# The skip term D times x of a state-space stage: from TensorE to GpSimd

## The chip, the cores and the metric

The kernel runs on one core of a Trainium2 chip. The metric is the device time of one execution in microseconds (us); less is better. The core has five engines that run their own instruction streams and meet at semaphores: PE (TensorE, matrix products), DVE (VectorE), ACT (ScalarE), POOL (GpSimd) and SP (SyncE, which issues most DMAs).

## The reference, cut to what matters

One layer of a hybrid diffusion backbone: attention beside a bidirectional Mamba-2 state-space mixer, then a feed-forward part. Only the mixer's output matters here. `xs` is the convolved input (length l, 8 heads of 64 values), `z` a gate:

```python
y_f, fin_f = ssd_chunked(xs, dt_f, a_f, bm, cm, init_f)
y_b, fin_b = ssd_chunked(flip(xs), flip(dt_b), a_b, flip(bm), flip(cm), init_b)
y = y_f + flip(y_b) + d_skip[:, None] * xs        # d_skip: one number per head
y = y.reshape(b, l, SSM_WIDTH) * silu(z)
return rms_norm(y, g_out), fin_f, fin_b
```

`ssd_chunked` splits the sequence into chunks of 128 tokens. A chunk's result has a part from inside the chunk (a 128x128 matrix of weights per head, times x) and a carried part (C times the state that enters the chunk, scaled by a decay per token). There are 1,024 latent tokens and 256 prompt tokens, so 10 chunks.

## The kernel before, in words

The stage is in `phase_front`. It works on one chunk `c` at a time, 0 to 9, with 128 tokens on the partitions and 512 channels (8 heads of 64) along the free axis. All arithmetic is float32. Each engine has its own loop over `c`, in an order written out by hand; there is no planner. The lines of the profile are those of kernel.py.

Before this loop there is a stage over the same chunks that makes the gate z (PE lines L373 to L375) and sweeps the backward state down the sequence. It ends with the semaphore `s_ready`, after which DVE, POOL and PE begin chunk 0.

**PE**, for chunk c: the carried parts, forward into bank A[1] and backward into A[2] (L1407, one semaphore `off_done` for both); the exponents of chunk c+1 (`segments`, L1368 and L1370); the chunk's contribution to the next state (L1347), which overwrites A[1] and so waits for `off_f_read`; the scores C B of chunk c+1 (L1391); then, after `y_ready` of chunk c-1, the four products of x with a diagonal matrix of D (L1419), which begin the sum in bank A[3]; eight products of the weights with x on top of them (L1422, `diag_done`); and the transposes of the normalised chunk c-1 (`y_turn`, L1376), which wait for ACT.

**DVE**, for chunk c: `yv` = A[1] times the forward decay (L1137); `off_b` = A[2] times the backward decay (L1139); `yv += off_b` (L1143); `next_state`, the decayed state plus A[1] (L1129), which waits for PE L1347 and for POOL's `decayed`; `weights_in_chunk` of chunk c+1, a sum and a product of 1,024 elements in a partition (L1116, which waits for ACT's exponential, and L1119); then `yv += A[3]` (L1150) and `yv *= z` (L1151), which gives `y_ready`. Of these, L1116, L1119, L1143 and L1151 have both inputs in SBUF; L1137, L1139, L1129 and L1150 have one in PSUM.

**POOL**, for chunk c: `weigh` (L696), x times the forward weights, free to start when PE has read the old one; `decay` (L675), which waits for `y_ready` of chunk c-1; `rstd` of chunk c-1 (L680 and L681, a power of one element); and `load_u` (L687), a DMA it issues itself.

**ACT**, for chunk c: the sum of squares of chunk c-1 (L860, after `y_ready`); the exponential of chunk c+1 (L871, after the exponents); a copy of the scores (L873); the scaling of chunk c-1 by `rstd` (L865, after POOL L681); and the copy of the transposed chunk back to SBUF (L877).

**SP** stores each finished chunk and loads rows for attention. When all engines are done, the attention phase begins.

The diagonal matrices `ddiag` are made by ACT, once, in the stage before (L845). `Chain.link` marks an instruction with a semaphore and makes its own engine wait for it.

Of the kernel before, what the change touches and what calls it, by code (L numbers as in the profile page):

```python
# [23 lines left out]
P = 128  # L24
# [3 lines left out]
ALU = mybir.AluOpType  # L28
ACT = mybir.ActivationFunctionType
# [6 lines left out]
NT = T // P  # L36
# [8 lines left out]
SH, SP_, DS = 8, 64, 128  # L45
SW = SH * SP_
# [3 lines left out]
N_XBC, N_Z = 8, 4  # L50
# [19 lines left out]

C_GPRE, C_GFFN, C_BMOD, C_GQ, C_GKV, C_CW, C_CB, C_GS, C_DB, C_AL, C_DS = 0, 8, 16, 64, 67, 69, 93, 101, 105, 121, 137
N_COLS = 141

# [312 lines left out]
def phase_front(L):  # L386
# [6 lines left out]
    with ExitStack() as st:  # L393
# [18 lines left out]
        def at(name, home, skip, shape, dt=F32):  # L412

            return nc.alloc_sbuf_tensor_at(name, shape, dt, offset=L.home[home] + skip)
# [9 lines left out]
        maskb = at("maskb", "conv_acc", 0, [P, 2, 4, P], BF16)  # L424
        ddiag = at("ddiag", "conv_acc", 2048, [P, 4, P])
        identb = at("identb", "conv_acc", 4096, [P, P], BF16)
# [30 lines left out]
        def turn_bank(n):  # L457
# [22 lines left out]
         s_ready, cb_done, cb_read, seg_done, exp_done, off_done, off_f_read, off_b_read, w_ready, diag_done, y_ready, squared,  # L480
         rstd_ready, yn_ready, y_turned, mix_ready, sf_ready, dec_ready, fin_mm, fin_cp, consts, pch) = (
             L.sem("ss_" + n) for n in (
                 "ones", "xwf_ready", "st_loaded", "st_turned", "sch", "z_done", "z_copied", "x_turned",
                 "x_copied", "xw_ready", "s_mm", "s_ready", "cb_done", "cb_read", "seg_done", "exp_done", "off_done",
                 "off_f_read", "off_b_read", "w_ready", "diag_done", "y_ready", "squared", "rstd", "yn_ready", "y_turned", "mix_ready",
                 "sf_ready", "dec_ready", "fin_mm", "fin_cp", "consts", "pch"))
        block = st.enter_context(nc.Block())
# [46 lines left out]
        per_head = lambda ap: ap.rearrange("p (a r) -> p a r", r=2).unsqueeze(3).to_broadcast([P, 4, 2, SP_])  # L534
        dskip = L.cols[:, C_DS:C_DS + 4]
        up2 = L.up2
# [19 lines left out]
        def _(sp):  # L556
# [39 lines left out]
            for d in range(2):  # L596
                sp.dma_start(st_in[:, d, :, :], L.dram["state_ssm"][0, 0, d].rearrange("(a h) p n -> (h p) a n", a=4)
                             ).then_inc(st_loaded, 16)

            sp.wait_ge(z_done, NT)  # L600
            for dst, name in ((L.table, "rope_table"), (L.wq_raw, "w_uq"), (L.wk_raw, "w_uk"), (L.wv_raw, "w_uv")):
# [18 lines left out]
        def _(pool):  # L620
# [72 lines left out]
            def weigh(c):  # L693

                pool.wait_ge(s_mm, NS + c)
                pool.tensor_tensor(heads4(quads(xw[:, 0, :])), heads4(xs(c)), per_head(wgt[:, c, 0:8]), ALU.mult  # L696
                                   ).then_inc(xwf_ready, 1)

            pool.wait_ge(s_ready, NS)
            for c in range(NT):  # L700
                weigh(c)
                decay(c)
                if c >= 1:
                    rstd(c - 1)
                if c + 2 < NT:
                    load_u(c + 2)
# [3 lines left out]
        def _(act):  # L710
# [118 lines left out]
            def constants(i):  # L829

                if i < 2:
                    act.activation(pick[0:64, i, :, :], across(L.const[0:64, K_SEL:K_SEL + 16], P), ACT.Copy,
                                   scale=-1.0).then_inc(consts, 1)
                elif i < 4:
                    d = i - 2
                    act.activation(maskb[:, d, :, :], L.const[:, K_MASK + d * P:K_MASK + (d + 1) * P]
                                   .unsqueeze(1).to_broadcast([P, 4, P]), ACT.Copy).then_inc(consts, 1)
                elif i == 4:
                    act.activation(identb[:], L.ident, ACT.Copy).then_inc(consts, 1)
                elif i == 5:  # L840
                    act.activation(up2[64:66, :], L.ones[64:66, 0:1].to_broadcast([2, T]), ACT.Copy
                                   ).then_inc(ones_set, 1)
                elif i == 6:
                    for a in range(4):
                        act.activation(ddiag[:, a, :], L.ident, ACT.Copy, scale=dskip[:, a:a + 1]).then_inc(consts, 1)  # L845

# [46 lines left out]
        def _(dve):  # L893
# [239 lines left out]
            for c in range(NT):  # L1133
# [7 lines left out]
                dve.wait_ge(off_f_read, c + 1)  # L1141
                dve.wait_ge(off_b_read, c + 1)
                f.link(dve.tensor_tensor(yv[:, c % 2, :], yv[:, c % 2, :], off_b[:], ALU.add))  # L1143

                if c + 1 < NT:
                    next_state(c)
                    weights_in_chunk(c + 1)

                dve.wait_ge(diag_done, c + 1)
                f.link(dve.tensor_tensor(yv[:, c % 2, :], yv[:, c % 2, :], A[3], ALU.add))  # L1150
# [8 lines left out]
        def _(pe):  # L1159
# [218 lines left out]

            pe.wait_ge(consts, 9)
            pe.wait_ge(ones_set, 1)  # L1380
# [19 lines left out]
            for c in range(NT):  # L1400
# [15 lines left out]
                if c >= 1:  # L1416
                    pe.wait_ge(y_ready, c)
                for a in range(4):
                    pe.matmul(A[3][:, chunk(a)], L.xbcT[:, a, chunk(c)], ddiag[:, a, :], start=(a == 0), stop=False)  # L1419
                pe.wait_ge(w_ready, c + 1)  # L1420
                for h in range(SH):
                    mm = pe.matmul(A[3][:, h * SP_:(h + 1) * SP_], wt[:, c % 2, h, :],  # L1422
                                   xs(c)[:, h // 2, (h % 2) * SP_:(h % 2 + 1) * SP_], start=False, stop=(h == SH - 1))
                mm.then_inc(diag_done, 1)
# [1874 lines left out]
```

## Time and profile before

| | us |
|---|---|
| median of 3 runs (1698.46 to 1698.77) | 1698.68 |
| the profiled execution, its time | 1697.26 |
| the profiled execution, its span | 1695.4 |
| PE busy | 1635.9 (96%) |
| DVE busy | 988.7 (58%) |
| ACT busy | 682.1 (40%) |
| POOL busy | 77.7 (5%) |

The profile is one execution. Times count from the start of its span. In a row of the timeline the first number is when an instruction began, the second how long it took; then the engine, the line, the operation, what it wrote and read, and its shape. An idle time that stood before it is in brackets, with what ended it. An instruction that began and then had to wait for something inside the chip shows a longer duration, not an idle time. PE's instructions overlap, so for PE the distance between two starts says more than a duration. In a row of the windows, each pair is an engine's busy time in that stretch and its count of instructions, in the order PE, weight loads of PE, DVE, ACT, POOL, followed by PE's granted clock as a share of 2.4 GHz, the DMA share and GB/s.

### The profile page before, as it was taken

How to read it: one execution, taken by the hardware profiler on the slowest of the kernel's cores; microseconds unless marked ns; L12 is line 12 of the kernel's file. 1: busy time of each engine (PE TensorE's matmuls, PEld its weight loads, DVE VectorE, ACT ScalarE, POOL GpSimd, SP SyncE). 2: the span in 40 equal slices, each digit the busy share in tenths (PEclk: the TensorE clock that was granted, in tenths of full speed). 3: DMA queues.
4: the chain of work that ended last, by engine and by line, in shares of the span. 5: the costliest groups of instructions: out<-in, count | busy, mean ns of one | idle time of the engine just before them, and what ended most of it. 6: DMA issues, size and time to landing. Idle time of an engine off the chain costs nothing. (4 is left out here: it accounts for less than half of the span.)

```text
span 1695.4 us, 24882 instructions
## 1 busy us (share of the span) xinstructions
PE 1635.9 (96%) x9795; PEld 1450.6 (86%) x9795; DVE 988.7 (58%) x1562; ACT 682.1 (40%) x1188; POOL 77.7 (5%) x116
## 2 busy tenths in 40 slices
PE   6899999999899999989999999999999999999997
PEld 4787878878788888878888999999999999888886
DVE  4653644258755645564588455545555555466788
ACT  4532112335543535454564333333333333434453
POOL 1101000034100000000100000000000000000011
PEclk9999999999999999999999999999999999999999
DMA  9323441013300000214312222222222225763355
GB/s 371 141 97 142 157 151 51 1 52 91 87 7 14 13 1 2 106 42 164 118 69 79 82 87 105 78 91 90 97 89 80 104 80 195 228 226 101 119 168 188
DMA packets 76291, 176.35 MB, mean 104 GB/s; under 512 B 10352, under 2 KB 26944, under 8 KB 74128
## 3 DMA queue, kind: packets, MB, share of 16 engines
q1 hardware_dynamic: 72080, 169.75, 28.9%
q0 software_dynamic: 4096, 5.01, 0.9%
q8 instruction: 79, 1.29, 0.3%
q14 instruction: 36, 0.29, 0.1%
HBM read 131.02 MB, written 43.70 MB: 103 GB/s over the span
## 5 line engine op out<-in xcount | busy, mean ns | idle before, releaser
L373 PE MATMUL psF<-gv,gu_ring 128*128 128x320 f32 x1224 | 379.3, 310 | 3.8 <-DVE gv L2659 3.1
L374 PE MATMUL psF<-gv,gu_ring 128*128 128x320 f32 x1224 | 378.8, 310 | 0.0
L375 PE MATMUL psF<-gv,gu_ring 128*128 128x320 f32 x1224 | 378.8, 309 | 0.0
L373 PEld LDWEIGHTS psF<-gv,gu_ring 128*128 128x128 f32 x1224 | 230.5, 188 | 4.7 <-issue 3.6
L374 PEld LDWEIGHTS psF<-gv,gu_ring 128*128 128x128 f32 x1224 | 230.4, 188 | 0.0
L375 PEld LDWEIGHTS psF<-gv,gu_ring 128*128 128x128 f32 x1224 | 230.4, 188 | 0.0
L373 PE MATMUL psF<-d_w_ring,d_hid_ring 128*128 128x512 f32 x360 | 140.2, 389 | 0.0
L374 PE MATMUL psF<-d_w_ring,d_hid_ring 128*128 128x512 f32 x360 | 140.1, 389 | 0.0
L375 PE MATMUL psF<-d_w_ring,d_hid_ring 128*128 128x512 f32 x360 | 140.0, 389 | 0.0
L373 PE MATMUL psP<-hT_hi,win_hi 128*128 128x512 f32 (+1 forms) x336 | 124.2, 370 | 2.7 <-DVEq L1064 1.5
L375 PE MATMUL psP<-hT_hi,win_lo 128*128 128x512 f32 (+1 forms) x336 | 119.6, 356 | 0.0
L374 PE MATMUL psP<-hT_lo,win_hi 128*128 128x512 f32 (+1 forms) x336 | 119.3, 355 | 0.0
L2459 ACT ACTIVATE hraw<-psF 128x320 f32<-128x320 f32 x130 | 56.6, 437 | 149.8 <-PE psF L375 147.4
L2709 DVE TENSOR_TENSOR hraw<-hraw,psF 128x320 f32<-128x320 f32 x132 | 63.4, 485 | 41.1 <-ACT hraw L2459 35.2
L1788 DVE TENSOR_TENSOR pt_lo<-psPT,pt_hi 128x512 fp32r<-128x512 f32 (+1 forms) x104 | 58.3, 581 | 40.7 <-ACT pt_hi L1664 40.7
L373 PEld LDWEIGHTS psF<-d_w_ring,d_hid_ring 128*128 128x128 f32 x360 | 67.6, 188 | 14.3 <-DVE hraw L2898 0.5
L2501 ACT ACTIVATE d_hid_ring<-d_hid 128x640 fp32r<-128x640 f32 x54 | 40.0, 740 | 98.7 <-PE psF L375 98.0
L374 PEld LDWEIGHTS psF<-d_w_ring,d_hid_ring 128*128 128x128 f32 x360 | 67.6, 188 | 14.1
L375 PEld LDWEIGHTS psF<-d_w_ring,d_hid_ring 128*128 128x128 f32 x360 | 67.6, 188 | 14.1
L2455 ACT ACTIVATE gu_ring<-raw_gu 128x512 fp32r<-128x512 f32 x65 | 40.9, 629 | 95.8 <-PE psF L375 95.8
L373 PEld LDWEIGHTS psP<-hT_hi,win_hi 128*128 128x128 f32 x336 | 63.8, 190 | 17.6 <-issue 4.6
L2766 DVE TENSOR_TENSOR d_hid_ring<-d_hid,d_hid_ring 128x640 fp32r<-128x640 f32 x54 | 44.5, 824 | 53.6 <-ACT d_hid_ring L2501 53.4
(434 smaller groups left out, 3385.7 us busy)
## 6 DMA issues: line engine op xcount, KB each, us to landing
hid_variants<-hraw SPq DMA_DIRECT2D x77, 320.0 KB, 2.2
d_hid<-hid_variants SPq DMA_DIRECT2D x58, 320.0 KB, 3.0
m_wring<-in_w_mod SPq DMA_DIRECT2D x16, 1024.0 KB, 4.9
d_b<-in_w_down SPq DMA_DIRECT2D x44, 256.0 KB, 4.2
win_raw<-in_w_in SPq DMA_DIRECT2D x18, 512.0 KB, 5.7
w_mod_staged<-in_w_mod SPq DMA_DIRECT2D x16, 512.0 KB, 14.7
d_hid_more<-hid_variants SPq DMA_DIRECT2D x19, 320.0 KB, 3.1
raw_gu<-in_w_gate SPq DMA_DIRECT2D x11, 512.0 KB, 3.9
```

What stands on the lines that cost most here:

```text
L373: pe.matmul(out, w_hi, x_hi, start=first, stop=False, skip_group_check=onto)
L374: pe.matmul(out, w_hi, x_lo, start=False, stop=False, skip_group_check=onto)
L375: return pe.matmul(out, w_lo, x_hi, start=False, stop=last, skip_group_check=onto)
L1788: dve.tensor_tensor(pt_lo[:, g[0]:g[-1] + 1, r:r + P], psPT[:, (g0 + i) % 2, 0:len(g), :], pt_hi[:, g[0]:g[-1] + 1, r:r + P].bitcast(F32), ...
L2455: act.activation(w_slot(q)[:, 0, :], block_of(r, n), ACT.Copy).then_inc(wv_hi, 1)
L2459: act.activation(dst[:, chunk(c)], psA(n, c), ACT.Copy).then_inc(copied, 1)
L2501: act.activation(ring_h(e, 0), hr[e % HR], ACT.Copy).then_inc(h_hi, 1)
L2709: dve.tensor_tensor(dst[:, chunk(c)], src[:, chunk(c)], bank(c), ALU.add).then_inc(added, 1)
L2766: dve.tensor_tensor(ring_h(e, 1), hr[e % HR], ring_h(e, 0).bitcast(F32), ALU.subtract).then_inc(h_lo, 1)
```

## The change

The four products with the diagonal matrix leave PE, and with them `ddiag` and ACT's four instructions that make it. POOL makes `dx` = D times x by two more operations of 512 elements in each chunk: `skip(c)`, the product, between `weigh(c)` and `decay(c)`, and `add_skip(c)`, which adds it onto `off_b` once DVE has written that. D is loaded by a small DMA of SP, eight numbers to every partition. On DVE, L1143 now waits for the sum (`skip_added`) and stands behind the next state and the next weights.

```diff
@@ SP @@
+            sp.wait_ge(conv_read, N_XBC)
+            sp.dma_start(dskip[:], L.dram["d_skip"].to_broadcast([P, 8])).then_inc(skip_loaded, 16)
             sp.wait_ge(z_done, NT)
@@ POOL @@
+            def skip(c):
+                p.link(pool.tensor_tensor(heads4(quads(dx[:])), heads4(xs(c)), per_head(dskip[:]), ALU.mult))
+            def add_skip(c):
+                pool.wait_ge(off_b_read, c + 1)
+                pool.tensor_tensor(off_b[:], off_b[:], dx[:], ALU.add).then_inc(skip_added, 1)
             pool.wait_ge(s_ready, NS)
+            pool.wait_ge(x_copied, 2 * NT)
+            pool.wait_ge(skip_loaded, 16)
             for c in range(NT):
                 weigh(c)
+                if c >= 1:
+                    pool.wait_ge(skip_added, c)
+                skip(c)
                 decay(c)
+                add_skip(c)
                 if c >= 1:
                     rstd(c - 1)
@@ ACT @@
-                elif i == 6:
-                    for a in range(4):
-                        act.activation(ddiag[:, a, :], L.ident, ACT.Copy, scale=dskip[:, a:a + 1]).then_inc(consts, 1)
@@ DVE @@
                 dve.wait_ge(off_f_read, c + 1)
-                dve.wait_ge(off_b_read, c + 1)
-                f.link(dve.tensor_tensor(yv[:, c % 2, :], yv[:, c % 2, :], off_b[:], ALU.add))
                 if c + 1 < NT:
                     next_state(c)
                     weights_in_chunk(c + 1)
+                dve.wait_ge(skip_added, c + 1)
+                f.link(dve.tensor_tensor(yv[:, c % 2, :], yv[:, c % 2, :], off_b[:], ALU.add))
                 dve.wait_ge(diag_done, c + 1)
@@ PE @@
                 if c >= 1:
                     pe.wait_ge(y_ready, c)
-                for a in range(4):
-                    pe.matmul(A[3][:, chunk(a)], L.xbcT[:, a, chunk(c)], ddiag[:, a, :], start=(a == 0), stop=False)
                 pe.wait_ge(w_ready, c + 1)
                 for h in range(SH):
-                    mm = pe.matmul(..., start=False, stop=(h == SH - 1))
+                    mm = pe.matmul(..., start=(h == 0), stop=(h == SH - 1))
```

The remaining edits take the columns of D out of the table `cols` (141 columns become 137) and give D its own input.

## Rows read from the trace of the kernel before

**Rows 1.** Windows: the z stage, the loop over chunks, the turn between them.

```profile
330.00:340.00 10.00, 10.00 (x51) 8.27 (x50) 2.07 (x3) 3.63 (x9) 0.00 (x0) 1.00 0.00 0
350.00:355.00 5.00, 3.64 (x11) 1.99 (x12) 1.72 (x3) 2.07 (x4) 0.00 (x0) 0.69 0.69 265
365.00:435.00 70.00, 69.95 (x464) 58.83 (x463) 58.38 (x72) 34.20 (x52) 30.28 (x41) 1.00 0.30 80
```

**Rows 2.** Timeline, PE, one turn of the loop: start, duration, engine, line, operation.

```profile
389.35 0.61 PE L1376 MATMUL psP<-const,yn 128*128 128x128 f32 x4
...
391.33 0.58 PE L1368 MATMUL psP<-pick,up 66*128 66x512 f32 x1
...
393.38 1.03 PE L1347 MATMUL psP<-xw,chunks_lo 128*128 128x256 f32 x4
...
394.69 1.06 PE L1419 MATMUL m_psC<-ddiag,xbcT 128*128 128x128 f32 x8
...
395.58 1.90 PE L1422 MATMUL m_psC<-chunks_hi,wt 128*128 128x64 f32 x16
...
397.32 0.60 PE L1376 MATMUL psP<-const,yn 128*128 128x128 f32 x4
```

**Rows 3.** Timeline, DVE, the same turn.

```profile
391.24 0.69 DVE L1151 TENSOR_TENSOR yv<-yv,chunks_hi 128x512 f32<-128x512 f32 x1
...
391.84 0.68 DVE L1137 TENSOR_TENSOR yv<-psP,dt_feats 128x512 f32<-128x512 f32 x1
...
392.44 0.68 DVE L1139 TENSOR_TENSOR off_b<-m_psM,dt_feats 128x512 f32<-128x512 f32 x1
...
393.23 0.70 DVE L1143 TENSOR_TENSOR yv<-yv,off_b 128x512 f32<-128x512 f32 x1
...
394.50 0.69 DVE L1129 TENSOR_TENSOR sf<-decayed,psP 128x512 f32<-128x512 f32 x1 [0.58 <-PE psP L1347]
...
395.55 1.60 DVE L1116 TENSOR_TENSOR wt<-seg 128x1024 f32<-128x1024 f32 x1 [0.36 <-ACT seg L871]
...
397.19 1.22 DVE L1119 TENSOR_TENSOR wt<-wt,cb 128x1024 f32<-128x1024 f32 x1
```

**Rows 4.** Timeline, POOL, the same turn.

```profile
392.07 1.04 POOL L675 TENSOR_TENSOR decayed<-sf,dt_feats 128x512 f32<-128x512 f32 x1 [3.82 <-DVE yv L1151]
...
393.47 0.88 POOL L681 TENSOR_TENSOR y_rs<-y_ms,y_nh 128x1 f32<-128x1 f32 x1
...
395.01 1.05 POOL L696 TENSOR_TENSOR xw<-chunks_hi,dt_feats 128x512 f32<-128x512 f32 x1
```

**Rows 5.** Timeline, ACT, the same turn.

```profile
392.50 0.19 ACT L860 ACTIVATION_READ_ACCUMULATOR yn<-yv 128x1 f32 x1
...
393.64 1.88 ACT L871 ACTIVATE seg<-psP 128x2048 f32<-128x2048 f32 x1 [0.96 <-PE psP L1370]
...
395.68 0.72 ACT L865 ACTIVATE yn<-yv,y_rs 128x512 f32<-128x512 f32 x1
```

**Rows 6.** Timeline, DVE and POOL, the start of chunk 0.

```profile
357.96 2.13 POOL L696 TENSOR_TENSOR xw<-chunks_hi,dt_feats 128x512 f32<-128x512 f32 x1 [70.28 <-DVEq L1108]
357.97 1.23 DVE L1116 TENSOR_TENSOR wt<-seg 128x1024 f32<-128x1024 f32 x1
...
359.23 1.95 DVE L1119 TENSOR_TENSOR wt<-wt,cb 128x1024 f32<-128x1024 f32 x1
...
360.06 2.02 POOL L675 TENSOR_TENSOR decayed<-sf,dt_feats 128x512 f32<-128x512 f32 x1
```

**Rows 7.** Timeline, DVE L1151 in chunks 0, 8 and 9.

```profile
367.15 0.69 DVE L1151 TENSOR_TENSOR yv<-yv,chunks_hi 128x512 f32<-128x512 f32 x1
...
430.54 0.69 DVE L1151 TENSOR_TENSOR yv<-yv,chunks_hi 128x512 f32<-128x512 f32 x1
...
435.00 0.69 DVE L1151 TENSOR_TENSOR yv<-yv,chunks_hi 128x512 f32<-128x512 f32 x1
```

**Rows 8.** Timeline, PE, the transposes of the last chunk.

```profile
438.26 0.63 PE L1376 MATMUL psP<-const,yn 128*128 128x128 f32 x4 [0.61 <-ACT yn L865]
```

More of the change, by code:

```diff
@@ L68 @@
 MOD_ALL = 6 * D // MOD_W
-C_GPRE, C_GFFN, C_BMOD, C_GQ, C_GKV, C_CW, C_CB, C_GS, C_DB, C_AL, C_DS = 0, 8, 16, 64, 67, 69, 93, 101, 105, 121, 137
-N_COLS = 141
+C_GPRE, C_GFFN, C_BMOD, C_GQ, C_GKV, C_CW, C_CB, C_GS, C_DB, C_AL = 0, 8, 16, 64, 67, 69, 93, 101, 105, 121
+N_COLS = 137
 K_ID, K_MASK, K_SEL, K_FOLD, K_TRI, K_SA, K_SB, K_MT, K_MD, K_SUM, K_SUM4 = 0, 128, 384, 400, 528, 656, 672, 672, 688, 704, 706
@@ L424, in phase_front @@
         maskb = at("maskb", "conv_acc", 0, [P, 2, 4, P], BF16)
-        ddiag = at("ddiag", "conv_acc", 2048, [P, 4, P])
+        dx = at("dx", "conv_acc", 2048, [P, SW])
         identb = at("identb", "conv_acc", 4096, [P, P], BF16)
@@ L480, in phase_front @@
          s_ready, cb_done, cb_read, seg_done, exp_done, off_done, off_f_read, off_b_read, w_ready, diag_done, y_ready, squared,
-         rstd_ready, yn_ready, y_turned, mix_ready, sf_ready, dec_ready, fin_mm, fin_cp, consts, pch) = (
+         rstd_ready, yn_ready, y_turned, mix_ready, sf_ready, dec_ready, fin_mm, fin_cp, consts, pch, skip_added, skip_loaded) = (
              L.sem("ss_" + n) for n in (
@@ L485, in phase_front @@
                  "off_f_read", "off_b_read", "w_ready", "diag_done", "y_ready", "squared", "rstd", "yn_ready", "y_turned", "mix_ready",
-                 "sf_ready", "dec_ready", "fin_mm", "fin_cp", "consts", "pch"))
+                 "sf_ready", "dec_ready", "fin_mm", "fin_cp", "consts", "pch", "skip_added", "skip_loaded"))
         block = st.enter_context(nc.Block())
@@ L534, in phase_front @@
         per_head = lambda ap: ap.rearrange("p (a r) -> p a r", r=2).unsqueeze(3).to_broadcast([P, 4, 2, SP_])
-        dskip = L.cols[:, C_DS:C_DS + 4]
+        dskip = at("d_skip", "conv_acc", 4576, [P, 8])
         up2 = L.up2
@@ L1377, in y_turn @@
                 mm.then_inc(y_turned, 1)
-            pe.wait_ge(consts, 9)
+            pe.wait_ge(consts, 5)
             pe.wait_ge(ones_set, 1)
@@ L1422, in _ @@
                     mm = pe.matmul(A[3][:, h * SP_:(h + 1) * SP_], wt[:, c % 2, h, :],
-                                   xs(c)[:, h // 2, (h % 2) * SP_:(h % 2 + 1) * SP_], start=False, stop=(h == SH - 1))
+                                   xs(c)[:, h // 2, (h % 2) * SP_:(h % 2 + 1) * SP_], start=(h == 0), stop=(h == SH - 1))
                 mm.then_inc(diag_done, 1)
@@ L3280 @@
             col(a["g_ssm_out"][0]), np.tile(a["dt_bias"].reshape(1, 16), (P, 1)),
-            np.tile(a["a_log"].reshape(1, 16), (P, 1)),
-            np.repeat(a["d_skip"][0].reshape(4, 2).T, P // 2, axis=0)], axis=1),
+            np.tile(a["a_log"].reshape(1, 16), (P, 1))], axis=1),
+        "d_skip": a["d_skip"].reshape(1, 8),
         "b_mod": a["b_mod"], "g_post_mix": a["g_post_mix"], "g_post_ffn": a["g_post_ffn"],
```

## The prediction

> **What bounds the kernel now.** I read the page first (PE is busy nearly throughout), then the chain that ended last, which reaches back only some tens of us into the feed-forward part and says nothing of this stage, then the windows of the stage, and then its timeline, engine by engine. In the loop PE is busy 69.95 of 70 us at full clock, DVE 58.38, ACT 34.20, POOL 30.28 [rows 1]. One turn takes 397.32 - 389.35 = 7.97 us on PE [rows 2]. From the end of chunk 0's L1151 (367.84) to chunk 8's (431.23) are 63.39 us, 7.92 a turn [rows 7]. PE waits for nothing; DVE waits 0.58 us for PE's L1347 and 0.36 for ACT's exponential, which itself waited for PE [rows 3, 5]. So PE sets the pace, and DVE is barely a microsecond behind it.
>
> **A second resource.** At the start of chunk 0 POOL's L696 and DVE's L1116 begin 0.01 us apart. L1116 takes 1.23 us, L696 2.13 against 1.05 later. Then L1119 takes 1.95 against 1.22, and POOL's L675 2.02 against 1.04 [rows 3, 4, 6]. Each that found the other running waited for it, and they took strict turns: whoever waited came before the other's next instruction. Counted back from their ends with the undisturbed durations, each began its work about 0.14 us before the other's end (359.05 against 359.20; 359.96 against 360.09; 361.04 against 361.18). L1116 and L1119 have both inputs in SBUF. L1137 and L1139, with one in PSUM, ran beside POOL's L675 at 0.68 and 1.04, undisturbed [rows 3, 4]. L1143 (both in SBUF, 393.23 to 393.93) held up POOL's power L681: 0.88 us, of which, counted from 393.79, 0.56 is its own [rows 3, 4]. The Trainium skill, page "SBUF — State Buffer", section "Who interferes with whom", states that a VectorE instruction with two SBUF inputs and a GpSimd one that reads SBUF exclude each other for the whole instruction. The trace agrees but for the 0.14 us; without these the sum below would be some 6 us larger.
>
> **The change, part by part.**
>
> PE loses L1419: 395.58 - 394.69 = 0.89 us a turn [rows 2]. Alone that makes its turn 7.97 - 0.89 = 7.08, and 10 of them would be worth 8.9 us. DVE's work doesn't shrink, so it becomes the bound: the question is its turn.
>
> ACT loses four small copies in the z stage, where PE is busy 10.00 of 10 us and ACT 3.63 [rows 1]: nothing. SP's DMA of D is issued after the last convolution, which is also what POOL waited for before its 70.28 us of idleness [rows 6]; SP then waits for the z stage as before. Its landing has 70 us: nothing, and if it were late it would cost just its lateness, once.
>
> POOL gets `skip` and `add_skip`. No row shows them. By the nearest, L696 and L675, each is 1.04 us; below that is nothing known, above it 2.13, the disturbed case, which is a wait and counted as one here. The Trainium skill, "GPSIMD Engine Reference", section 3.1, has a two-input operation on GpSimd 1.96 times as long as on VectorE, which by an estimate from 0.69 us would be 1.35; the rows of this kernel say 1.04, and by the page the sum below would be about 6 us larger.
>
> POOL's work is then 4 x 1.04 + 0.36 + 0.56 + 0.66 (its DMA, 395.01 - 394.35), about 5.8 us a turn: it isn't the bound. But it and DVE's four two-SBUF instructions (1.23 + 1.22 + 2 x 0.69 = 3.83) now take turns.
>
> **One turn, worked out.** Zero is the end of L1151 of chunk c-1 (391.93 in the rows). Offsets from the rows: L1137 starts at -0.09, L1139 ends at 1.19; POOL's `decay` 0.14 to 1.18. `add_skip` needs L1139: 1.19 + 0.14 = 1.33 to 2.37. The power starts 0.36 after the operation before it: 2.73. ACT is done with the squares at 0.76 (392.69), so its exponential runs 0.78 to 2.66 if PE is early; L1116 could start at 2.69. PE's L1347 needs L1137: 0.68 to 1.71, and L1129 starts 0.09 later, 1.80 to 2.49 [rows 2 to 5]. Without L1143 ahead of it L1129 is early; the exponential is what comes last.
>
> *Short turn (PE early).* L1116 2.69 to 3.92, ahead of the power by 0.04. The power works 3.78 to 4.34. L1119 would start at 3.95, works 4.20 to 5.42. `weigh` would start at 5.00, works 5.28 to 6.33. L1143 would start at 5.34, works 6.19 to 6.88. `skip` 6.74 to 7.79. L1150 6.91 to 7.60. L1151 would start at 7.63, works 7.65 to 8.34. Turn: 8.34 us. Meanwhile the late power holds up ACT's scaling (4.38 to 5.10) and PE's transposes (5.20), and from these to the next L1347 are 393.38 - 389.35 = 4.03 us: 9.23, that is 0.89 of the next turn and not 0.68. PE is late.
>
> *Long turn (PE late).* The exponential starts 0.26 after L1347: 1.15 to 3.03, L1116 could start at 3.06, and the power, 2.73 to 3.29, is there first. L1116 works 3.15 to 4.38, `weigh` 4.24 to 5.29, L1119 5.15 to 6.37, `skip` 6.23 to 7.28, L1143 7.14 to 7.83, L1150 7.86 to 8.55, L1151 8.58 to 9.27. Turn: 9.27 us. Here the transposes start at 4.15, the next L1347 could start at 8.18, long before 9.27 + 0.68: PE is early again, and waits 1.77 us.
>
> So short and long alternate: four each from chunk 1 to 8, 4 x 8.34 + 4 x 9.27 = 70.44 us against 63.39: **+7.05**.
>
> **Chunk 0.** L696 to 360.09 as now. `skip` takes the place of L675, 360.06 to 362.08; `decay`, linked, 362.16 to 363.20; L1129 363.25; `add_skip` to 364.27; L1116 works 364.13 to 365.36, `weigh` 365.22 to 366.27, L1119 366.13 to 367.35, `skip` 367.21 to 368.26, L1143 368.12 to 368.81, L1150 to 369.53, L1151 369.56 to 370.25, against 367.84 [rows 6, 7]: **+2.41**.
>
> **The end.** Chunk 9 has no weights to make: L1139 to 1.19, `add_skip` to 2.37, L1143 2.42 to 3.11, L1150 from 3.14, L1151 from 3.86 to 4.55, against 435.69 - 431.23 = 4.46 [rows 7]: **+0.09**. L1143 holds the power until 2.97, so scaling ends at 4.29, the transposes of chunk 8 start at 4.39, L1347 at 4.83, L1129 ends at 6.64, and the last transposes, behind eight more of 0.11 us, start at 7.62, that is 3.07 after L1151; now it is 438.26 - 435.69 = 2.57 [rows 7, 8]: **+0.50**, between 0 and 1.
>
> After that all engines meet, so what the stage loses is lost. Sum: 7.05 + 2.41 + 0.09 + 0.50 = 10.05. The profile's span goes from 1695.4 to 1705.4. Its own time, 1697.26, is 1.4 under the median, so I add the sum to the median: 1698.68 + 10.05 = **1708.7 us**, +0.59%.
>
> **Rivals.**
>
> *The other side: no collisions.* If the two new operations don't hold DVE up, the short turn is L1116 2.69, L1119 3.95, L1143 5.09, L1150 5.81, L1151 6.53 to 7.22; the turn after it, with PE late, 7.66; mean 7.44. Eight turns give -3.9, chunk 0 (only the delayed L1129) +0.66, the end +0.59: -2.6, 1696.0, within the 0.2% (3.4 us) that a measurement of this kernel can tell from no change. For it: PE really is relieved. Against it: rows 6. It decides once fewer than about two of the five handovers in a turn cost DVE their 0.8 us.
>
> *Only long turns.* The short one hangs on L1116 beating the power by 0.04 us. If it never does: 8 x 9.27 = 74.16, +10.77 + 3.0 = 13.8, 1712.5.
>
> *Only short turns.* If the scaling doesn't hold PE up (0.21 us): 8 x 8.34 = 66.72, +3.33 + 3.0 = 6.3, 1705.0.
>
> *The clock.* Between the z stage and the loop PE is busy 3.64 of 5 us and the granted clock is 0.69, so part of it at 1.2 GHz [rows 1]. In long turns PE waits 1.77 us. At half speed L1347 would take 1.03 us more, and L1116 start some 0.5 to 0.8 later; four to eight times, that is 2 to 6 us on top: 1711 to 1715. Against it: the row is of one longer gap.
>
> **How the numbers follow.** Chances: alternating turns 0.55, only long 0.13, only short 0.11, the clock 0.08, no collisions 0.09, a part of them (1699 to 1703) 0.04. An error of 0.05 us in a handover, some four a turn, is 1.6 us, so the likeliest case alone is 1706.5 to 1711. The range, 1703 to 1715 us, holds all but the last two cases and a tail of the clock. Slower by over 0.2%: 0.86. Within: 0.10. Faster by over 0.2%: 0.04, a no-collision case in which PE is early in every turn.
>
> **What would show it.** Right: no L1419; L1119 and L1143 much longer than 1.22 and 0.69 in most turns, with POOL's L696 or the new product beside them; turns of 8.3 and 9.3; L1116 at 1.23 when it precedes the power; PE idle before L1347, with DVE's L1137 named. Wrong: L1143 at 0.69 everywhere and turns of 7.2 to 7.7; or new POOL operations far from 1.04 us; or DVE's L1143 waiting for POOL, not colliding with it; or a granted clock under 1 in the loop.

## The result and the profile after

| | before | after |
|---|---|---|
| median of the runs, us | 1698.7 (1698.46 to 1698.77) | 1715.89 (1714.59 to 1718.27) |
| the profiled execution, its time and span, us | 1697.26, 1695.4 | 1716.44, 1714.6 |

The changed kernel is slower by 1.1%: the ratio is 1.011, 95% interval 1.0098 to 1.0121. Predicted were 1708.7 us and at most 1715. The direction was right, the size was not, and the median lies just above the range.

The page after, its first lines. POOL's busy time has grown from 77.7 to 107.6 us, and PE's, which lost the 40 products with the diagonal matrix (80 matmuls in the profile, 9795 to 9715), has not shrunk:

```profile
span 1714.6 us, 24753 instructions
## 1 busy us (share of the span) xinstructions
PE 1638.4 (96%) x9715; PEld 1447.7 (84%) x9715; DVE 998.7 (58%) x1562; ACT 680.6 (40%) x1184; POOL 107.6 (6%) x136
```

The windows after: the loop (against the last row of [rows 1]), one long turn's neighbourhood microsecond by microsecond, and the end of the loop:

```profile
365.00:435.00 70.00, 56.35 (x320) 44.12 (x319) 57.70 (x60) 28.17 (x42) 48.72 (x51) 0.95 0.24 64
...
377.00:378.00 1.00, 1.00 (x6) 0.91 (x7) 1.00 (x1) 0.37 (x1) 1.00 (x2) 0.70 0.19 17
378.00:379.00 1.00, 1.00 (x4) 0.81 (x3) 0.97 (x2) 0.22 (x1) 1.00 (x1) 0.50 0.00 0
379.00:380.00 1.00, 1.00 (x4) 0.72 (x4) 0.74 (x2) 0.20 (x1) 0.28 (x2) 0.50 0.39 112
380.00:381.00 1.00, 1.00 (x4) 0.62 (x2) 0.00 (x0) 0.53 (x2) 0.98 (x1) 0.59 0.53 151
381.00:382.00 1.00, 1.00 (x6) 0.44 (x6) 0.99 (x2) 0.00 (x0) 0.00 (x0) 1.00 0.00 0
...
450.00:460.00 10.00, 5.60 (x26) 4.30 (x26) 4.14 (x7) 4.20 (x8) 2.56 (x5) 0.70 0.25 68
```

PE is now idle for 13.65 of 70 us in the loop, and its granted clock, 1.00 before, averages 0.95. It is not low evenly: between 377 and 381 it stands at 0.50, the 1.2 GHz level, and at 381 it is back at 2.4 GHz.

The timeline of DVE after, one short turn (371.59 to 379.77) and the long one behind it (to 391.68), to be set beside [rows 3]:

```profile
373.47 0.69 DVE L1143 TENSOR_TENSOR sf<-decayed,psP 128x512 f32<-128x512 f32 x1 [0.68 <-PE psP L1360]
374.38 1.23 DVE L1130 TENSOR_TENSOR wt<-seg 128x1024 f32<-128x1024 f32 x1 [0.21 <-DVE sf L1143]
375.64 1.23 DVE L1133 TENSOR_TENSOR wt<-wt,cb 128x1024 f32<-128x1024 f32 x1
376.78 1.54 DVE L1161 TENSOR_TENSOR yv<-yv,off_b 128x512 f32<-128x512 f32 x1
378.36 0.69 DVE L1163 TENSOR_TENSOR yv<-yv,m_psC 128x512 f32<-128x512 f32 x1
379.08 0.69 DVE L1164 TENSOR_TENSOR yv<-yv,chunks_hi 128x512 f32<-128x512 f32 x1
381.01 0.69 DVE L1151 TENSOR_TENSOR yv<-psP,dt_feats 128x512 f32<-128x512 f32 x1 [1.24 <-PE m_psM L1420]
...
384.84 3.54 DVE L1130 TENSOR_TENSOR wt<-seg 128x1024 f32<-128x1024 f32 x1 [0.36 <-ACT seg L885]
388.41 1.22 DVE L1133 TENSOR_TENSOR wt<-wt,cb 128x1024 f32<-128x1024 f32 x1
389.55 0.68 DVE L1161 TENSOR_TENSOR yv<-yv,off_b 128x512 f32<-128x512 f32 x1
```

The lines have moved: L1130 and L1133 are the weights (L1116 and L1119 before), L1143 the next state (L1129), L1151 and L1153 the carried parts (L1137, L1139), L1161 the addition of `off_b` (L1143), L1164 the gate (L1151). The addition takes 1.54 us in the short turn, where it was 0.70. In the long turn the same addition is undisturbed, but L1130 takes 3.54.

POOL in the same stretch, to be set beside [rows 4]; L698 is `weigh`, L703 the new product, L708 the new sum, L683 the power, L689 the DMA:

```profile
372.87 1.27 POOL L708 TENSOR_TENSOR off_b<-off_b,dx 128x512 f32<-128x512 f32 x1
374.24 0.18 POOL L682 TENSOR_SCALAR y_ms<-y_ss 128x1 f32<-128x1 f32 x1
374.50 1.53 POOL L683 TENSOR_TENSOR y_rs<-y_ms,y_nh 128x1 f32<-128x1 f32 x1
375.99 0.69 POOL L689 DMA_DIRECT2D pick<-u_scratch  x1
376.71 1.06 POOL L698 TENSOR_TENSOR xw<-chunks_hi,dt_feats 128x512 f32<-128x512 f32 x1
377.73 1.49 POOL L703 TENSOR_TENSOR dx<-chunks_hi,d_skip 128x512 f32<-128x512 f32 x1
...
384.53 0.68 POOL L689 DMA_DIRECT2D pick<-u_scratch  x1
385.24 1.06 POOL L698 TENSOR_TENSOR xw<-chunks_hi,dt_feats 128x512 f32<-128x512 f32 x1
386.24 1.04 POOL L703 TENSOR_TENSOR dx<-chunks_hi,d_skip 128x512 f32<-128x512 f32 x1
```

And PE, to be set beside [rows 2]; L1360 is the contribution to the state, L1389 the transposes, L1420 the carried parts:

```profile
372.25 1.13 PE L1360 MATMUL psP<-xw,chunks_lo 128*128 128x256 f32 x4 [2.07 <-DVE yv L1151]
...
376.93 0.66 PE L1389 MATMUL psP<-const,yn 128*128 128x128 f32 x4 [1.37 <-ACT yn L879]
377.40 1.90 PE L1420 MATMUL psP<-sf,xbcT 128*128 128x256 f32 x4
379.10 1.88 PE L1420 MATMUL m_psM<-chunks_lo,xbcT 128*128 128x256 f32 x4
```

The chain that makes a long turn still longer can be read off these rows. In the short turn PE waits twice, 2.07 us for DVE and 1.37 for the scaling, which stands behind POOL's power, which stood behind DVE's L1130. Then its clock falls, and the two L1420 take 1.90 and 1.88 us. At full clock they take 1.03. DVE's L1151, the first of the next chunk, waits 1.24 us for the second of them.

From the end of L1164 in one chunk to its end in the next, chunks 0 to 9, the turns are 8.18, 11.91, 8.17, 9.49, 8.17, 11.90, 8.11, 10.71 and 4.80 us. So they alternate, as predicted, but three of the four long ones are 1.2 to 2.4 us longer than the fourth, 9.49.

### The profile page after: what moved, and what is told of

It reads as the page before. It is cut to its first block and busy times, and to the rows that moved or that the text cites. A ratio compares the mean times of both kernels' runs of the same rounds, so it can differ in the third digit from the quotient of the medians.

```text
span 1714.6 us, 24753 instructions
## 1 busy us (share of the span) xinstructions
PE 1638.4 (96%) x9715; PEld 1447.7 (84%) x9715; DVE 998.7 (58%) x1562; ACT 680.6 (40%) x1184; POOL 107.6 (6%) x136
```

## The experiments

All ratios are to the kernel before, run on the same chip. In three of them, e1, e5 and e10, the term D times x is left out of the result; in e9 and e11 a part of it is lost in chunk 0. All else is computed whole.

**e1: neither of the two operations** (D times x left out). PE is relieved, and DVE's order is the new one.

```diff
@@ POOL @@
                 weigh(c)
-                if c >= 1:
-                    pool.wait_ge(skip_added, c)
-                skip(c)
                 decay(c)
-                add_skip(c)
@@ DVE @@
-                dve.wait_ge(skip_added, c + 1)
+                dve.wait_ge(off_b_read, c + 1)
```

> This kernel is the changed one without the product and the sum on GpSimd: the term D times x is left out of the output. PE's relief and the new order on DVE stay. Theory A (the new GpSimd work costs its turns at a port shared with DVE, and the waits it makes let PE's clock fall): granted clock 1.00 in the loop, no instruction over 2 us on DVE; GpSimd's weigh still meets L1133, so a turn is 7.2 + 0.74 = 7.96 us, no shorter than the 7.92 of before, and the kernel takes 1698 to 1700 us (up to 1702 if the later start of the changed kernel, 2.8 us in its first 50 us, belongs to it). Theory B (no port; the time is lost in waits for GpSimd's queue): turns of 7.1 to 7.5, 1694 to 1696 us.

1699.86 us, ratio 1.0018 (1.0008 to 1.0027): the kernel before, with 0.89 us less on PE in each chunk, is no faster, rather 0.2% slower. The turns are 8.25, 8.23, four of 8.22, 7.80 and 7.51, the clock is 1.00. DVE, with `weigh` in its way:

```profile
377.10 0.69 DVE L1139 TENSOR_TENSOR sf<-decayed,psP 128x512 f32<-128x512 f32 x1 [0.68 <-PE psP L1356]
378.00 2.13 DVE L1126 TENSOR_TENSOR wt<-seg 128x1024 f32<-128x1024 f32 x1 [0.21 <-DVE sf L1139]
380.16 1.23 DVE L1129 TENSOR_TENSOR wt<-wt,cb 128x1024 f32<-128x1024 f32 x1
```

`weigh` began at 377.98, 0.02 us ahead, and costs L1126 0.90 us. In [rows 3, 4] it begins 0.54 us ahead of the weights and costs them 0.38. So an earlier DVE only runs further into `weigh`. The two new operations cost the rest: 1715.89 - 1699.86 = 16.0 us (15.8 against e2 below, the changed kernel in all that matters, which ran on the same chip as e1).

**e10: e1 with the addition of `off_b` back in its old place** (D times x left out).

```diff
@@ DVE @@
                 dve.wait_ge(off_f_read, c + 1)
+                dve.wait_ge(off_b_read, c + 1)
+                f.link(dve.tensor_tensor(yv[:, c % 2, :], yv[:, c % 2, :], off_b[:], ALU.add))
                 if c + 1 < NT:
                     next_state(c)
                     weights_in_chunk(c + 1)
-                dve.wait_ge(off_b_read, c + 1)
-                f.link(dve.tensor_tensor(yv[:, c % 2, :], yv[:, c % 2, :], off_b[:], ALU.add))
```

> The first experiment with L1143 of before back at its old place on DVE (yv += off_b ahead of the next state); the term D times x is left out of the output. If the move of that sum also cost something (behind L1133 it lengthens the part of the turn that follows ACT's exponential, while ahead of the next state it lies in DVE's wait for it): turns of 7.1 to 7.5 us against the 8.22 of the first experiment, 1691 to 1695 us. If the move was free: as the first experiment, 1698 to 1702.

1694.89 us, ratio 0.9991 (0.9979 to 1.0003). The turns are 7.81 us where e1's are 8.22. In the new place the addition costs 0.41 us a turn even with nothing to wait for, because it no longer fills DVE's 0.68 us of waiting for PE's contribution. The turns of 7.1 to 7.5 us that were expected didn't come: `weigh` still costs the first weights 1.07 us (2.30 against 1.23).

**e3: the changed kernel with PE kept busy.** Four products of x with the identity stand where the products with the diagonal stood; the first of the weights' products overwrites them.

```diff
@@ PE @@
+                for a in range(4):
+                    pe.matmul(A[3][:, chunk(a)], L.xbcT[:, a, chunk(c)], L.ident, start=(a == 0), stop=(a == 3))
                 pe.wait_ge(w_ready, c + 1)
```

> The changed kernel with four dead products back on PE at their old place (x times the identity, overwritten at once by the products of the weights); the output is complete. Theory A with the clock as part of the loss: PE is busy 0.9 us more a turn, the granted clock stays at or near 1.00, turns alternate between 8.2 and about 9.5 and none takes 11 to 12; 1708 to 1712 us. Rival (the clock is a symptom that costs nothing): as the changed kernel, 1715 to 1717, or slower.

1707.41 us, ratio 1.0051 (1.0034 to 1.0068). Work that is thrown away makes the changed kernel 8.5 us faster (8.3 against e2, on the same chip). Its loop in the windows, and the two kinds of turn on DVE:

```profile
365.00:435.00 70.00, 64.35 (x408) 52.20 (x407) 59.49 (x65) 31.62 (x47) 55.26 (x55) 1.00 0.28 74
```

```profile
372.91 1.22 DVE L1130 TENSOR_TENSOR wt<-seg 128x1024 f32<-128x1024 f32 x1 [0.21 <-DVE sf L1143]
374.17 1.22 DVE L1133 TENSOR_TENSOR wt<-wt,cb 128x1024 f32<-128x1024 f32 x1
375.31 1.54 DVE L1161 TENSOR_TENSOR yv<-yv,off_b 128x512 f32<-128x512 f32 x1
...
377.60 0.69 DVE L1164 TENSOR_TENSOR yv<-yv,chunks_hi 128x512 f32<-128x512 f32 x1
...
381.68 1.23 DVE L1130 TENSOR_TENSOR wt<-seg 128x1024 f32<-128x1024 f32 x1 [0.37 <-ACT seg L885]
382.94 1.95 DVE L1133 TENSOR_TENSOR wt<-wt,cb 128x1024 f32<-128x1024 f32 x1
384.81 1.53 DVE L1161 TENSOR_TENSOR yv<-yv,off_b 128x512 f32<-128x512 f32 x1
```

The granted clock is 1.00 throughout the loop, and the turns are 8.17 and 9.49 us, strictly in turn until the last short one (8.12): eight make 70.55 us, where the prediction had 70.44. The changed kernel shows the same 8.17 and 9.49 where its own clock stayed at 1.00 (391.7 to 409.3). So the fallen clock, with what it sets off, makes up nearly all of the difference between forecast and result.

**e5: the new operations only write** (D times x left out). Each is replaced by two memsets of the same tile, together 1.1 us.

```diff
@@ POOL @@
-                p.link(pool.tensor_tensor(heads4(quads(dx[:])), heads4(xs(c)), per_head(dskip[:]), ALU.mult))
+                p.link(pool.memset(dx[:], 0.0))
+                p.link(pool.memset(dx[:], 0.0))
...
-                pool.tensor_tensor(off_b[:], off_b[:], dx[:], ALU.add).then_inc(skip_added, 1)
+                p.link(pool.memset(dx[:], 0.0))
+                pool.memset(dx[:], 0.0).then_inc(skip_added, 1)
```

> The changed kernel with each of GpSimd's two new operations replaced by two memsets of the same 512 elements, with the same waits and signals; the term D times x is left out of the output. GpSimd is as busy and as late, but these instructions read nothing from SBUF. Theory A: DVE's L1161 takes 0.69 us beside them and L1133 is held only by weigh; turns of 8.3 to 8.5, 1702 to 1706 us. Theory B (GpSimd's queue is late, whatever it does): 1713 to 1717 us, as the changed kernel.

1706.39 us, ratio 1.0048 (1.003 to 1.0066). The time is a little above what was expected. The waits and the time on POOL are nearly those of the change. Six of the eight turns are 8.11 to 8.16 us; the two others, 9.43 and 9.96, have a fallen clock in or before them. That none is 9.49 at full clock needn't come from what the memsets leave unread. Two of them end 0.17 us sooner than the sum does, so POOL's power begins 2.73 us into the turn (400.49), 0.06 ahead of the weights and not behind them, and neither holds the other up. What e5 shows of the reading lies in single rows. The rows of DVE and of POOL:

```profile
375.68 2.46 DVE L1132 TENSOR_TENSOR wt<-seg 128x1024 f32<-128x1024 f32 x1 [0.21 <-DVE sf L1145]
378.17 1.23 DVE L1135 TENSOR_TENSOR wt<-wt,cb 128x1024 f32<-128x1024 f32 x1
```

```profile
376.98 0.53 POOL L703 MEMSET dx<- 128x512 f32 x1
377.57 0.52 POOL L704 MEMSET dx<- 128x512 f32 x1
```

L1132 had to wait for `weigh` (375.99 to 377.04). Counted back from its end, its own 1.23 us began at 376.91, so both memsets lie inside them, and neither side is longer for it. In the changed kernel the product, in the place of these memsets, waits for DVE (1.49 against 1.04). The addition tells nothing here: its 1.54 us in the changed kernel's short turn are a wait for `weigh`, which in e5 falls to the weights instead.

So it is POOL's reading that collides, not its being busy. The Trainium skill, page "SBUF — State Buffer", section "Who interferes with whom", says just this: a VectorE instruction with two SBUF inputs contends with a GpSimd one that reads SBUF, not with one that only writes. The trace agrees: 0.53 and 0.52 us beside DVE for the memsets, 1.49 for the product.

**e2: the table of 141 columns kept**, the last four zero.

```diff
-N_COLS = 137
+N_COLS = 141
...
-            np.tile(a["a_log"].reshape(1, 16), (P, 1))], axis=1),
+            np.tile(a["a_log"].reshape(1, 16), (P, 1)), np.zeros((P, 4), np.float32)], axis=1),
```

> The changed kernel with the table of columns padded from 137 back to 141 columns (zeros that nobody reads), so that its DMA and all tiles behind it lie where they did. If the later start (2.8 us within the first 50 us of the profile) comes from the new table: 1712 to 1714 us and no later start. If it is chance between executions or comes from elsewhere: 1715 to 1717 us.

1715.69 us, ratio 1.0101 (1.0078 to 1.0123): no different from the changed kernel. The table plays no part. Its profile has three turns of 11.9 to 12.0 us, each behind a fallen clock. Twice the fall came 1.1 and 1.5 us (estimates from windows of 1 us) after the end of PE's first wait (2.02 and 2.31 us, up to 369.27 and 389.40), before there was a second one, and the eight products that followed took 3.52 and 3.47 us instead of 1.90.

**e8 and e13: POOL's DMA moved**, from its place behind `rstd`, to find what the 3.54 us of L1130 are worth. In e8 it stands behind `decay`, in e13 behind the product.

```diff
@@ e8 @@
                 decay(c)
+                if c + 2 < NT:
+                    load_u(c + 2)
                 add_skip(c)
@@ e13 @@
                 skip(c)
+                if c + 2 < NT:
+                    load_u(c + 2)
                 decay(c)
@@ both @@
                     rstd(c - 1)
-                if c + 2 < NT:
-                    load_u(c + 2)
```

> The changed kernel with GpSimd's own DMA (L689) between decay and add_skip, not right ahead of weigh; complete output. In the profile of the changed kernel two L1130 took 3.54 us: each had begun some 0.3 us into that DMA and got the port only after weigh and the product, two GpSimd instructions in a row. If it is the DMA that keeps DVE out: no L1130 over 2.4 us. The clock may still fall, so a long turn takes about 10.5 to 11.5 instead of 11.9, the kernel 1 to 3 us less than the changed one. If DVE simply loses two turns whatever GpSimd did before: L1130 of 3.5 us again and no gain.

> The changed kernel with GpSimd's DMA behind the product skip, where GpSimd waits for y_ready anyhow; complete output. Theory A: no L1130 over 2.2 us; the power still comes behind the sum and still meets L1130, so PE still waits and the clock still falls; turns of 8 and 9 to 11, 1709 to 1716 us. Rival (the DMA's place is the whole trouble): 1703 or less.

e8: 1719.07 us, ratio 1.0127 (1.0112 to 1.0143), the slowest of all, where a gain was expected. The 3.54 is gone inside the turns, and the short turn is down to 7.55 us, but three long ones are 11.36, 12.67 and 12.80, each behind a fallen clock. And in chunk 0 L1130 takes 4.00. The power comes later and meets DVE earlier, twice in a row:

```profile
375.55 1.25 POOL L682 TENSOR_SCALAR y_ms<-y_ss 128x1 f32<-128x1 f32 x1
376.88 1.56 POOL L683 TENSOR_TENSOR y_rs<-y_ms,y_nh 128x1 f32<-128x1 f32 x1
```

PE has waited 3.37 us before and 1.37 after, and the loop's clock is 0.93. e13: 1713.8 us, ratio 1.0096 (1.0081 to 1.0112). Its long turns are 9.40, 10.92 and twice 9.49. Its eight turns are 71.98 us against 76.64 of the change, but L1130 takes 3.34 in chunk 0, which costs 1.3 us there, and a clock that fell in the last short turn makes chunk 9 6.12 us instead of 4.80. So the median is only 2.1 us under that of the change (1.9 against e2, on another chip). The move shifted such waits more than it removed them, and what the 3.54 alone is worth stays open.

**e6: the product made in the z stage**, into `dxc(c)`, the place of x's transposed copy, `L.xbcT[:, 0:4, chunk(c)]`, which nobody reads any more; in the loop POOL only adds.

```diff
@@ POOL, before the loop @@
+                pool.tensor_tensor(heads4(dxc(c)), heads4(xs(c)), per_head(dskip[:]), ALU.mult).then_inc(skip_made, 1)
...
+            for i in range(NT):
+                skip(i)
@@ POOL, in the loop @@
                 weigh(c)
-                if c >= 1:
-                    pool.wait_ge(skip_added, c)
-                skip(c)
                 decay(c)
                 add_skip(c)
```

> D times x is made by GpSimd for all chunks in the z stage, where GpSimd had nothing to do, into the four eighths of xbcT that nobody reads any more; in the loop only the sum add_skip is left. Complete output. Theory A: the product costs a turn at the port in each chunk, so L1161 is 0.69 to 0.9 us, chunk 0 is 2 us shorter, turns are 7.9 to 8.3, and with PE waiting less the clock mostly stays; 1700 to 1705 us. Theory B (the wait for the sum is what counts): no better than 1710.

1710.48 us, ratio 1.0074 (1.0061 to 1.0088). With one of the two operations gone the normal turns are 8.17 and 8.64, and 5.4 us come back. One turn of 12.33 is left, behind a fallen clock. Theory A had expected 1700 to 1705 us; the sum alone is enough to keep the two kinds of turn.

**e9: ACT fills the bank.** The product is made as in e6. ACT copies it into A[3] in PSUM, PE adds the weights' products on top, and DVE has its old order. Nothing of D times x is left in the loop on POOL or DVE. (In chunk 0 a part of the copy is lost.)

```diff
@@ ACT @@
+            def fill(c):
+                if c >= 1:
+                    act.wait_ge(bank_read, c)
+                act.activation(quads(A[3]), L.xbcT[:, 0:4, chunk(c)], ACT.Copy).then_inc(bank_filled, 1)
...
@@ PE @@
-                if c >= 1:
-                    pe.wait_ge(y_ready, c)
+                pe.wait_ge(bank_filled, c + 1)
...
-                    mm = pe.matmul(..., start=(h == 0), stop=(h == SH - 1))
+                    mm = pe.matmul(..., start=False, stop=(h == SH - 1), skip_group_check=True)
```

> A version meant to beat both: D times x made by GpSimd in the z stage, then copied by ACT into bank A[3] as soon as DVE has read it, and the products of the weights added onto it by PE (start=False); DVE in the order of before; no new GpSimd instruction in the loop. Complete output. Theory A: the turn is set by PE (7.1) or by ACT's exponential, turns of 7.1 to 7.5 us, the granted clock near 1.00, 1691 to 1695 us. Rival (ACT's copy delays its squares and the exponential by 0.6 us in each turn): turns of 7.7 to 8.0, no faster than before.

1696.38 us, ratio 1.0000 (0.999 to 1.0009). The turns of 7.1 to 7.5 us that theory A had didn't come. PE is relieved of 0.89 us a turn and DVE has no more work than before, and still six of the eight turns are 7.92 to 7.96 us. DVE and POOL show why:

```profile
380.99 2.30 DVE L1134 TENSOR_TENSOR wt<-seg 128x1024 f32<-128x1024 f32 x1 [0.21 <-DVE sf L1147]
```

```profile
380.44 0.68 POOL L689 DMA_DIRECT2D pick<-u_scratch  x1
381.15 1.06 POOL L698 TENSOR_TENSOR xw<-chunks_hi,dt_feats 128x512 f32<-128x512 f32 x1
```

L1134 begins while POOL issues its DMA, 0.16 us before `weigh`, and yet ends 2.30 later: less its own 1.23, it got the port at 382.06, 0.15 before the end of `weigh`. It lost 1.07 us, more than PE had gained. In the last two turns it began behind `weigh` instead and took 1.62 and 1.58, and these turns are 7.18 and 7.21 us.

**e11: e9 with the DMA right behind `weigh`**, and the bank wholly written once before the loop (a part of D times x is still lost in chunk 0). **e12: the kernel before with the same move of the DMA and nothing else.**

```diff
@@ POOL, e11 and e12 @@
                 weigh(c)
+                if c + 2 < NT:
+                    load_u(c + 2)
                 decay(c)
                 if c >= 1:
                     rstd(c - 1)
-                if c + 2 < NT:
-                    load_u(c + 2)
```

> The previous version mended for chunk 0 (PE writes the whole bank A[3] once before ACT fills it first), and with GpSimd's own DMA moved from ahead of weigh to behind it, where DVE is not waiting. Complete output. Theory A (a DVE instruction with two SBUF inputs that arrives during GpSimd's DMA waits for it and for the GpSimd instruction behind it too): L1134 falls from 2.30 us to 1.2 to 1.6, turns from 7.93 to 7.1 to 7.4, granted clock 1.00, so 4 to 6 us less than before: 1691 to 1694 us where before takes 1697. Rival (PE or ACT's exponential has become the bound at 7.9): turns of 7.9, no change.

> The kernel before with the same move of GpSimd's DMA and nothing else: how much of the previous one's gain belongs to the move. PE sets the pace of the kernel before (7.92 a turn, busy throughout), so theory A: L1116 is shorter, turns stay at 7.9, within 0.1% of before. If it gains 3 us or more, the pace was DVE's.

e11: 1695.23 us, ratio 0.9982 (0.9973 to 0.9992), turns of 7.2 us as expected, the time 1.2 us above what was. e12: 1697.84 us, ratio 1.0003 (0.9992 to 1.0014), turns of 7.94: there PE is the bound, and a smoother DVE is worth nothing. The two steps pay only together.

What the move changes isn't only when the DMA is issued: `weigh` starts 0.7 us earlier in the turn too. And e12 shows that a DMA issue by itself doesn't keep DVE out. Here L1116 begins 0.08 us into one (387.63 to 388.31), behind which POOL has nothing ready that reads, and takes no longer than alone, as in five other turns:

```profile
387.71 1.23 DVE L1116 TENSOR_TENSOR wt<-seg 128x1024 f32<-128x1024 f32 x1 [0.36 <-ACT seg L871]
```

So the theory with which e11 was built, that DVE waits for the DMA and for the instruction behind it, doesn't hold as it stands.

**e14: e11 with the bank first written as one group of products**, which makes D times x whole in every chunk.

```diff
@@ PE, before the loop @@
-                mm = pe.transpose(A[3][:, chunk(a)], L.ident, L.ident)
+                mm = pe.matmul(A[3][:, chunk(a)], L.ident, L.ident, start=(a == 0), stop=(a == 3))
```

> The kernel with the product made before the loop, ACT filling the bank, PE adding on top and POOL's DMA behind weigh, now with the bank written before the loop as one group of four products, so that nothing of D times x is lost. This changes four small products outside the turns. Both theories (the port, the clock) expect the turns of that kernel: 7.2 us, L1133 at 1.6 us or less, PE without waits and the granted clock at 1.00 in the loop. Time: 0.1% to 0.3% under the kernel before (1692 to 1695 us where that has 1697.6). If the gain had come from what was left out of chunk 0, the time would be that of the kernel before.

1693.42 us against 1698.06 of the kernel before, ratio 0.998 (0.997 to 0.9991): the one version with the whole result that is faster than both, by 0.2% against the kernel before. A turn on DVE, 7.22 us from one L1168 to the next:

```profile
386.75 1.58 DVE L1133 TENSOR_TENSOR wt<-seg 128x1024 f32<-128x1024 f32 x1 [0.21 <-ACT seg L881]
388.37 1.23 DVE L1136 TENSOR_TENSOR wt<-wt,cb 128x1024 f32<-128x1024 f32 x1
389.51 0.68 DVE L1166 TENSOR_TENSOR yv<-yv,m_psC 128x512 f32<-128x512 f32 x1
390.34 0.69 DVE L1168 TENSOR_TENSOR yv<-yv,chunks_hi 128x512 f32<-128x512 f32 x1
```

Eight turns take 426.65 - 369.01 = 57.64 us, against 63.39 in [rows 7]: -5.75. Chunk 0 takes 10.88 us against 9.87 [rows 6, 7] and loses 1.01 again: its first L1133 comes 0.01 us behind `weigh` and takes 2.11, where L1116 took 1.23. The median gains 4.6.

## Why the prediction was wrong in size

The terms, as increases over the kernel before, each from one profiled execution (e3's took 1709.93 us, 2.5 above its median). A turn ends with the gate on DVE; the end is the time from there to the last transposes.

| term | predicted | after | e3 (clock 1.00) |
|---|---|---|---|
| chunk 0 | +2.41 | +2.55 | +2.55 |
| eight turns | +7.05 | +13.25 | +7.16 |
| chunk 9 | +0.09 | +0.34 | +0.34 |
| the end | +0.50 | +1.86 | +0.97 |
| sum | +10.05 | +18.00 | +11.02 |

The loop also began 1.20 us later after (359.17 against 357.97 in [rows 6]); with it the sum is the whole difference of the spans, 19.2. In e3 it began 0.27 earlier. What moves that start between executions wasn't tried one by one. After e3's loop 1.95 us of its 12.7 are not accounted for.

**The step that failed is the rival called "The clock".** It had the right cause (PE's waits) and the right sign, and was set aside at 0.08: "Against it: the row is of one longer gap." The sum of 10.05 us has no term for it. The runs showed 7.0 us in its place: what the changed kernel has beyond e3, 6.1 in the eight turns and 0.9 at the end. The text had itself named a granted clock under 1 in the loop as a sign that it was wrong.

First, the chance was too low. PE's wait for DVE was foreseen (1.77 us), its second one, for ACT in the same turn, was not weighed with it. The four short turns have waits of 2.07 and 1.37, 2.30 and 1.36, 1.55 and 1.37, 2.31 and 1.32 us; the clock fell in all but the second. In e2 it fell twice behind the first wait alone. So the length of the waits doesn't tell which falls, and what does isn't settled. The Trainium skill, "TensorE: Matmul & The Clock Gate", section "HAM oscillation — how this bites in real kernels", tells of a kernel whose TensorE waits for a DMA in each round and starts the next one at the low clock. The trace agrees in part: the clock fell in three short turns of four, behind waits for DVE and ACT, but only 0.3 to 0.7 us (an estimate from windows of 1 us) after PE had begun again.

Second, the place and the price were off: 0.5 to 0.8 us for a fall, through L1347. That instruction, now L1360, takes 1.13 us in the short turns (372.25), as at full clock in e3; the slow ones are the two L1420 behind it, which hold up DVE's first instruction. Set against e3's 9.49, the turn of 11.91 lost 2.42 us. L1151 begins 1.31 later behind the slow L1420, the next state another 0.38 later, which is the clock itself, 1.69. L1130 and L1133 then take 1.58 longer and L1161 0.85 less: 0.73 more, because a DVE that is late begins L1130 0.40 us before `weigh`, and waits out `weigh` and the product both. So a fall changes the order at the port as well. 2.42 + 0 + 2.41 + 1.22 = 6.05 us is nearly all of the 6.09 that the eight turns have beyond e3, and the end has 0.89 beyond e3's, at a granted clock of 0.70.

**What was right.** DVE becomes the bound; POOL and DVE take turns at a port; the handover lies some 0.14 us before the other's end. That the turns are strict holds for e3's loop, not everywhere: the L1130 of 3.54 us let two instructions of POOL go first. Chunk 0 was off by 0.14. The alternation and its reason, the scaling behind the power behind the weights, are in the trace: L1130 at 374.38, the power at 374.50, a margin of 0.12 us where 0.04 was forecast, and PE idle before L1360 with DVE's L1151 named.

**What was right by two errors.** A short turn was forecast at 8.34 and took 8.17: the power was to hold up L1133 by 0.25 us. In e3 it began at 373.03 and took 1.53, so its own 0.56 lay from 374.00 to 374.56; L1133 began inside it, at 374.17, and took 1.22. The long turn was forecast at 9.27 and took 9.49, since a shorter short turn leaves PE further behind: 0.17 goes over, and 0.14 comes from later transposes; 0.09 of these 0.31 had been in the forecast as a wait for the power. The mean was 8.80 and is 8.83.

**A size that was off, and luck with it.** `add_skip` takes 1.27 us, not 1.04; the product, with D spread out over its heads, takes 1.04 undisturbed. The power, which follows the sum, begins 2.91 us into e3's short turn, where the forecast had 2.73, and L1130 at 2.79, where it had 2.69. With a sum of 1.04 us the power would by an estimate from these rows have begun at 2.68, ahead of L1130. So that L1130 came first, on which the short turn of the forecast hangs, came true only because a duration was wrong too. In e5 the power does come first, by 0.06 us: neither waits for the other, and the turns stay at 8.16.

**Rivals.** "No collisions" falls with the rows of the changed kernel and of e3. Its price was wrong too: 7.44 us a turn. With both operations removed the turn is 8.22 (e1), since `weigh` collides as well and the moved addition costs 0.41. "Only long" and "only short turns" are out by the alternation.

## What to carry to other kernels

When a change takes work from the engine that sets the pace, work out what its idle gaps do to its clock before pricing anything else, and read the price of low clock off the instruction that the next stage waits for, not off the one that you expect to be slow. To tell a clock loss from other causes, put useless work into the gap: here that gave 8.5 us back. Taking load off the engine that sets the pace pays only as far as the second engine can follow, and that engine's order against its port partner must then be set anew: PE's relief was worth nothing (e1, e9) until a DMA issue, and with it the start of `weigh`, had been moved (e14), and that move alone was worth nothing too (e12).

## What the runs showed of the hardware

- An instruction of DVE with two SBUF inputs that begins shortly before one of POOL's that reads SBUF can lose more than one turn. Begun 0.15 to 0.40 us ahead of `weigh`, while POOL issued a DMA (0.68 us), it waited through `weigh` (2.30 us in e9, 2.46 in e5, against 1.23 alone) and, with the product next, through that too (3.54). Begun while the sum ran, with no DMA between the sum and `weigh`, it waited through the rest of the sum, `weigh` and the product (4.00 in chunk 0 of e8, 3.34 in that of e13). Begun beside `weigh` itself, it got its turn behind it (1.58 us in e14, 1.95 in e3). And begun 0.08 us into a DMA with nothing ready behind it, it wasn't held up (1.23 in six turns of e12). What decides between these isn't settled.
- POOL's power of one element holds the port for a short part of its 0.56 us at most: in e5 L1132 (400.55, 1.22) ran beside it (400.49, 0.57) undisturbed, though the power itself has to wait for a DVE instruction that was first.
- POOL's memsets (0.52 us for 512 elements) and DVE's two-input instructions don't disturb each other: in e5 two of them (376.98, 377.57) ran inside L1132's own 1.23 us.
- Of two-input operations of 512 elements on POOL, one with a small second input spread out took 1.04 us, one with two full inputs 1.27, with DVE at 0.69 for either.
- The granted clock fell to 0.50 behind waits of 2.07 and 1.37 us in one turn of the changed kernel, behind a single one of 2.02 in e2, and stayed at 1.00 behind 2.30 and 1.36. In the changed kernel PE had worked from 372.25 to 375.56 between its two waits. It was back at 1.00 after about 4 us there, about 7 in e2.
- PE can add onto what ACT wrote into a PSUM bank, if the bank was first written by one group of products that PE started once (e14). When four transposes, each starting anew, had written it, part of ACT's data was lost (e11); that this was in the first chunk is inferred, since only there does the copy follow what e14 changed.
